# Decoder block on eight cores: the first attention chunk multiplies with values seven items behind its scores, with eight exponent tiles of its own

## What is computed

```python
z = x @ w_in                                  # q, k, v | pool | gates
q, k = rope(q), rope(k)                       # 8 heads of 64
# each query attends to its own block of 256 keys (causally) and to the
# 3 past blocks with the largest q . mean(k of the block)
y_attn = softmax(masked q k / 8) @ v
y_pool = multiscale_pool(u) @ w_branch_pool   # trailing means over 2, 4, 8, 16 tokens
x = layer_norm(alpha * x + (g_attn * (y_attn @ w_a) + g_pool * y_pool) @ w_out)
x = layer_norm(alpha * x + conv_ffn(x))
```

## Time and profile before

| | us |
|---|---|
| median of three runs | 965.54 (965.23 to 967.13) |
| the profiled execution | 966.26 |
| its span on the slowest core, core 6 | 964.7 |
| spans of the other cores | 961.0 to 963.8 (core 0) |
| PE busy, of the span | 931.1 (97%) |
| DVE busy | 586.1 (61%) |
| ACT busy | 459.1 (48%) |
| POOL busy | 227.5 (24%) |

### The profile page before, as it was taken

The page is one execution under the profiler, slowest core; times in us unless marked ns, Lnnn a source line. Parts: engine busy times, 40 slices in busy tenths (PEclk is TensorE's granted clock), DMA queues, the critical chain, the costliest instruction groups (busy, mean ns, idle before and its releaser), DMA issues.

```text
span 964.7 us, 16930 instructions; the slowest of 8 cores (961.0 to 964.7 us)
## 1 busy us (share of the span) xinstructions
PE 931.1 (97%) x5014; PEld 475.5 (49%) x5014; DVE 586.1 (61%) x1055; ACT 459.1 (48%) x839; POOL 227.5 (24%) x233
## 2 busy tenths in 40 slices
PE   4998998999999999999999999999999999999996
PEld 1454554666666654444444444444444444444443
DVE  6949754663433343665478787862877666664756
ACT  2275576777777742346445655551004555553000
POOL 5634544411111112545123232210000000000000
PEclk9999999999999999999999999999999999999999
DMA  8963100431213258574465744597325544540221
GB/s 138 186 130 59 54 1 24 82 74 37 56 34 60 46 126 143 142 171 114 131 131 138 153 115 88 113 219 139 132 88 148 93 86 68 85 69 1 104 93 66
DMA packets 30970, 94.95 MB, mean 98 GB/s; under 512 B 4880, under 2 KB 8336, under 8 KB 30240
## 3 DMA queue, kind: packets, MB, share of 16 engines
q0 software_dynamic: 12688, 52.70, 32.4%
q1 hardware_dynamic: 18192, 41.17, 13.1%
HBM read 125.11 MB, written 16.78 MB: 147 GB/s over the span
## 4 chain that ended last, share of the span: by engine, by line
PE 92%; DVE 3%; issue 2%; DMA 1%; ACT 1%; POOL 1%; DVEq 0%; ACTq 0%; POOLq 0%
PE ps L419 91%; DMA xT<-xT 1%; PE ps L423 1%; POOL P L439 1%; DVE hT L439 0%; DVE t L439 0%; ACT cbuf L436 0%; DVE row L452 0%; DVE cbuf L452 0%; DVE PT L859 0%; ACT abuf L436 0%; DVE row L439 0%; ACT PT L436 0%; ACT gbuf L436 0%; DVE PLt L452 0%
## 5 line engine op out<-in xcount | busy, mean ns | idle before, releaser
L419 PE MATMUL ps<-x1T,wgu 128*128 128x512 bf16 x1408 | 310.9, 379 | 3.8 <-DVE hT L439 2.1
L419 PEld LDWEIGHTS ps<-x1T,wgu 128*128 128x128 bf16 x1408 | 137.2, 98 | 170.8 <-issue 7.7
L452 DVE SCALAR_TENSOR_TENSOR cbuf<-abuf,small,cbuf 128x512 f32<-128x512 f32 x176 | 145.4, 827 | 100.0 <-ACT cbuf L436 90.0
L436 ACT ACTIVATE PT<-ps 128x512 bf16<-128x512 f32 (+1 forms) x288 | 154.1, 572 | 85.2 <-PE ps L419 76.7
L419 PE MATMUL ps<-xT,wm 128*128 128x512 bf16 x512 | 126.2, 379 | 0.0
L419 PE MATMUL ps<-PT,Vp 128*128 128x256 bf16 (+1 forms) x584 | 106.3, 265 | 4.4 <-DVE PT L859 4.3
L419 PE MATMUL ps<-q,k 72*128 72x256 bf16 x576 | 107.2, 267 | 0.2
L436 ACT ACTIVATE abuf<-ps 128x512 f32<-128x512 f32 x88 | 52.3, 595 | 109.8 <-PE ps L419 109.8
L410 POOL DMA_DIRECT2D wgu<-wgu x44 | 23.9, 544 | 292.4 <-PE ps L419 292.1
L439 POOL TENSOR_TENSOR mix<-m,m 128x512 bf16<-128x512 f32 x32 | 41.6, 1298 | 176.0 <-DVE m L452 171.6
L419 PE MATMUL ps<-wdb,hT 128*128 128x512 bf16 (+1 forms) x363 | 80.6, 373 | 0.0
(11 more groups left out here) (111 smaller groups left out, 1036.3 us busy)
## 6 DMA issues: line engine op xcount, KB each, us to landing
wgu<-wgu POOLq DMA_DIRECT2D x44, 512.0 KB, 6.1
wm<-wm POOLq DMA_DIRECT2D x16, 768.0 KB, 8.8
xres<-x SPq DMA_DIRECT2D x16, 512.0 KB, 4.5
x1s<-row SPq DMA_DIRECT2D x16, 512.0 KB, 3.0
row<-x1s SPq DMA_DIRECT2D x16, 512.0 KB, 9.6
out<-row SPq DMA_DIRECT2D x32, 256.0 KB, 2.0
wda<-wd POOLq DMA_DIRECT2D x5, 512.0 KB, 8.5
wdb<-wd POOLq DMA_DIRECT2D x3, 768.0 KB, 21.5
```

The costliest lines, as they stand in the source:

```text
L419: S.op("pe", lambda e: e.matmul(out, lhsT, rhs, start=start, stop=stop), reads=[lhsT, rhs], writes=[out])
L436: S.op("act", lambda e: e.activation(out=out, in_=in_, func=func, **kw), reads=rd, writes=[out])
L452: S.op(eng, lambda e: e.scalar_tensor_tensor(out=out, in0=in0, scalar=scalar, in1=in1, op0=op0, op1=op1), reads=rd, writes=[out])
```

## The change

The first chunk's items get eight exponent tiles of their own, `PTa0` to `PTa7`, at 124 to 132 KB of the arena, and their products are made seven steps behind the scores. The other chunks keep six tiles and a distance of five. A counter `nxt` says which product is due. At the change of chunk, step 30 makes the products of items 23, 24 and 25, after it has issued the exponent of item 30.

```diff
     PT = [T(f"PT{i}", [128, 512], BF16, PT0 + i * KB) for i in range(6)]
+    PTa = [T(f"PTa{i}", [128, 512], BF16, (124 + i) * KB) for i in range(8)]
...
-    LAG = 5
+    LAG = {0: 7, 1: 5, 2: 5, 3: 5}
...
+        def pbuf(i):
+            return PTa[i % 8] if items[i][0] == 0 else PT[i % 6]
...
-            pt = PT[i % 6]
+            pt = pbuf(i)
...
+        nxt = 0
...
-            if i >= LAG and pv(i - LAG):
-                ready.append(i - LAG)
+            while nxt <= i - LAG[items[nxt][0]]:
+                if pv(nxt):
+                    ready.append(nxt)
+                nxt += 1
...
-        for i in range(n - LAG, n):
+        for i in range(nxt, n):
```

## The result

The changed kernel takes 975.03 us in the median of four runs, the kernel before 965.40: a ratio of 1.0089, with a 95% interval of 1.0075 to 1.0103. One of the four, at 1058.92 us, was in a slower state of the chip and is left out of the ratio; the median of the other three is 974.52. The change is slower by 8.6 us (7.2 to 9.9). 972.9 was forecast, inside a range from 966.8 to 977.

What follows compares the result with a forecast made beforehand. PE is busy 97% of the span, so only its own waiting can be won. Core 0: 963.8 + 4.3 + 1.6 + 2.3 = 972.0, then + 1.56 - 0.7 = 972.9 us; range 966.8 to 977.

Steps and rivals of the forecast that it cites:

- The sum: Whole span: core 0 at 963.8 + 4.3 + 1.6 + 2.3 = 972.0 us, 972.9 on the scale of the median.
- Part 1: First chunk's early exponents wait for DMAs reading the staging tiles: 4.3 us on core 0, 2.2 on core 6.
- Part 2: After the exponents' wait on core 0, a stretch at 1.2 GHz costs 1.6 us, with ends 0 and 1.7.
- dearer: Rival: a second lower-clock stretch near 82 us, or masks beside POOL; 976 to 979 us, chance 0.08.
- Part 3: First-chunk products and norms two steps later: 2.05 - 0.5 + 0.8 = +2.3 us.
- the walk: DVE's queue from mask 12: DVE idles 2.3 us for POOL, norm 11 and rope pairs end later; +2.05 us.
- the wait of 2.05 us for the second pair: First chunk: the q tile begun at 84.85 needs the bank the second rope pair frees, until 86.9; +2.05 us.
- The order pays: Rival: exponents wait for staging, but part 3 is the plain gain of -2.9 us; 967.7 us, chance 0.18.
- the bytes are free in time: Rival: staging pieces land before the exponents overwrite them, with the plain gain; 962.7 us, chance 0.06.

Runs made afterwards that it cites:

- e1: Changed kernel with the distance back at five in the first chunk, its eight tiles still over the staging bytes; ratio 1.0063 to the kernel before.
- e7: Changed kernel with the first eight items in free tiles, the staging bytes used only from item 8 on; ratio 1.0029 to the kernel before.
- e2: Changed kernel with distance seven kept, its eight tiles being the six old ones and two in unused bytes; ratio 1.0019 to the kernel before.
- e9: e2 with the three DVE operations of the first chunk's g = 3 pooling fix left out; ratio 1.0002 to the kernel before.
- e6: e3 with the first chunk's g = 3 pooling fix and its matmul each one projection tile later; ratio 1.0023 to the kernel before.
- e4: e3 with the first chunk's g = 3 pooling fix one projection tile later in DVE's queue; ratio 1.0020 to the kernel before.
- e3: e2 with the products of items 21, 22 and 23 made together at step 28; ratio 1.0027 to the kernel before.

## Why the prediction was right

**Direction and size.** Slower, as forecast: +8.6 us (7.2 to 9.9) by the ratio, against +7.4 (972.9 over the 965.54 it started from). That it came this close is partly luck. The sum was made on core 0, 972.0, and core 0 took 968.1. The slowest, core 4, took 972.9 with other terms: PE's waits behind the first scores up to 200 us grew from 7.8 to 13.3 us and its time at 0.50 from 3.4 to 17.1 us, up to 6.8 us of work, together enough for the 10.8 us by which it is later at its first matmul with `wgu`.

**Part 1** held. The exponents waited for the staging DMAs, by name; PE's wait was 2.9 us on core 0, 3.8 on core 1, 4.2 on core 4 and 4.5 on core 6, against 4.3 predicted for core 0 and 2.2 for core 6. Which core suffers most isn't fixed: the pieces' landings scatter by execution. On core 0 the second four of k took 13.4 to 14.7 us before and 9.2 to 12.0 after, and core 0, which I took for the slowest, became the fastest. On core 6 they had all landed by 56.1 before and by 60.9 after, so that k held it and not q, as the prediction had it. e1 and e7 show the cause from both sides: the tiles alone bring the wait, and using the same bytes eight items later takes it away.

**Part 2** is the term that was mis-sized. I took 1.6 us for one stretch of 3.4 us at the lower clock after the exponents' wait. Behind that wait six of the eight cores had 3.4 or 6.8 us at 0.50, 4.3 us on average over the eight. Behind the waits for norm 11 and the first rope pair all eight had 3.4 or 6.8 us more, 5.5 on average, and for these the sum has nothing: only the rival "dearer" named a second stretch near 82 us. It came, and the time stayed under that rival's 976. Between 50 and 200 us the traces show 11.9 us at 0.50 per core, and 3.4 before; at half speed that is up to (11.9 - 3.4) / 2 = 4.3 us. PE's waits behind the first scores grew by 5.4 us per core, which leaves 3.2 of the 8.6 us of traced delay. So the clock cost some 3.2 to 4.3 us, where 1.6 was taken. e1 and e2 add to 7.4 us of traced delay and to 7.3 us more at 0.50, the change has 8.6 and 8.5; with one execution of each, that the combination costs more than its parts isn't shown.

**Part 3** came out in the walk's order: PE waits 2.7 us for norm 11, 1.1 for the first rope pair and 1.28 for exponent 30 (0.8 predicted), and for no mask before items 12 and 15. e2 gives the price alone: +1.8 us by the ratio, +2.4 on core 1, against +2.3 in the sum. But the sum is made of waits only, and in e2 core 1's waits grew by 1.2 us; the rest is the clock behind them, so that the two numbers agree is luck in part. The largest term, the wait of 2.05 us for the second pair, didn't show. In the changed kernel PE was at the lower clock just then and needed the time anyway (pair done at 92.58 + 0.67 = 93.25, tile begun at 93.97), so the walk's wait became slow work. In e9, at full clock, it is there as 1.6 us, and in e6, where the fix stands in front of the second pair, as 3.9.

**The cause behind part 3** was named too narrowly. The walk blames POOL's chain at the head of DVE's queue. e4 and e6 take the norm out from behind it and gain nothing; e9 takes the fix out and gains 1.6 to 2.9 us against e2, no more than brings it level with before. DVE had little slack here before the change; the third busy time is its own, 20.77 of 22.70 us on core 6:

```profile
70.10:92.80 22.70, 19.00 (x124) 10.52 (x123) 20.77 (x44) 12.66 (x30) 9.10 (x9) 1.00 0.32 59
```

So I read the runs like this: DVE's work in its order bounds this stretch, the longer distance moves PE ahead of DVE, and PE gives the time back at the next bank that it needs, with the lower clock on top where the wait comes in one piece. That the wait moved each time is shown: from 50 to 200 us, without the first q, PE waits 7.9 us per core before and 8.5 to 9.3 in the six runs with distance seven and no staging wait (e2, e3, e4, e6, e7, e9). That DVE's load is the reason is argued, since no run made DVE's work shorter and left everything else in place. What e3 to e6 don't settle is whether any order of this queue lets distance seven win; four orders were tried (e2, e3, e4, e6) and none did. A distance of six wasn't tried.

**The rivals.** "The order pays" falls by e2, "the bytes are free in time" by e1 and by the landings. The Trainium skill's fixed cost of about 2 us for a DMA (DMA: Bandwidth & Descriptors, Latency and other measured facts) would have led to the latter; here the pieces took 11.0 to 12.7 us on core 4, and the measurement decides.

## What to carry to other kernels

Before laying a new tile over old bytes, look up when the last reader's DMA lands, not when it is issued: here the gap was 9 to 15 us, and a tile free "by program order" held ACT for 5 us. Before lengthening a software pipeline to remove an engine's waits, look at who is late: if the producer's queue is full, a longer distance only lets the consumer run into the next resource that the same queue frees, and everything tied to the later result (here a norm and its accumulator) moves too. And price each new wait with the clock behind it: on this kernel 3.2 to 4.3 of the 8.6 us were work done at 1.2 GHz.

## What the runs showed of the hardware that was not expected

A stretch at the lower clock was either 3.4 or 6.8 us long. After one wait of 2.5 us or of 4.9 us (e1, core 1) it was 3.4; in the changed kernel, with 3.86 us on core 4 after a first wait of 0.35 us, and again with 2.67 and 1.10 us close together, it was 6.8 both times. The waits don't decide it alone: in e2 the same two, 2.7 and 1.1 us, were followed by 3.4 us on four cores and by 6.8 on the other four. What does decide was not tried. Core 0 of the changed kernel waited 2.89 us for its exponent, up to 61.33, and kept the full clock then, which goes far to make it the fastest core (3.4 us at 0.50 up to 200 us in all, 17.1 on core 4); its stretches from there:

```profile
61.40:87.00 25.60, 20.78 (x135) 11.68 (x137) 17.54 (x38) 16.90 (x40) 11.56 (x11) 1.00 0.22 44
87.20:90.50 3.30, 3.30 (x11) 1.46 (x12) 2.96 (x7) 0.60 (x1) 0.00 (x0) 0.50 0.37 74
```

A mask takes 0.28 us by itself, and 1.05 or 1.06 us behind the second rope pair, where POOL multiplies beside it. On core 4 of the changed kernel:

```profile
92.81 2.55 POOL L440 TENSOR_TENSOR kst<-t,t 128x512 bf16<-128x512 f32 x2 [9.04 <-DVE t L440]
...
93.18 1.06 DVE L863 TENSOR_TENSOR PTa<-PTa,tri 128x256 bf16<-128x256 bf16 x1
```

The mask starts 0.37 us into the first of POOL's two multiplications, which ends at 92.81 + 1.27 = 94.08, and itself ends 0.16 us later. POOL at work beside a mask isn't enough, though: on core 6 before, the mask at 67.72 began 0.08 us after one of POOL's additions and took 1.13 us, and the one at 68.77 began 0.07 us before the next and took 0.28. For masks that slide beside POOL's work it seems to matter which of the two starts first. It isn't a rule: one mask, at 126.25 on the same core, began 0.28 us after an addition and took 0.28 us.
